# Expert items turned: the last output product behind the next gather, a loop without a drain, the scatter in halves, and part of the routing behind the first gather

## The reference, cut to what matters

```python
def moe_swiglu(xn, w_router, w_gate, w_up, w_down):
    logits = (xn @ w_router).astype(jnp.float32)
    top_v, top_i = lax.top_k(logits, TOP_K)
    top_w = jax.nn.softmax(top_v, axis=-1)
    gates = jnp.sum(jax.nn.one_hot(top_i, N_EXPERTS, dtype=jnp.float32) * top_w[..., None], axis=-2)
    y = jnp.zeros_like(xn)
    for e in range(N_EXPERTS):
        y = y + gates[..., e:e + 1] * swiglu(xn, w_gate[e], w_up[e], w_down[e])
    return y
...
        h = h + moe_swiglu(xn, ...)
        h = h + per_layer_embedding(h, p[i], norm_ple[i], w_ple_up[i], w_ple_gate[i])
```

## Time and profile before

| | |
|---|---|
| median of 3 executions | 2706.61 us (2705.66 to 2718.25) |
| the profiled execution, its own time | 2699.85 us |
| its span, first to last instruction | 2698.0 us |
| mean granted TensorE clock | 0.98 |
| TensorE matmul busy | 2526.2 us, 94% of the span |
| VectorE busy | 1883.0 us, 70% |
| ScalarE busy | 1465.1 us, 54% |
| experts, first expert product to the first product of the next layer | 643.5 to 1693.0 us |

### The profile page before, as it was taken

One profiled execution on the slowest core, in us unless ns is written; L12 is line 12 of the kernel. 1 busy time (PEld: TensorE's weight loads), 2 busy tenths in 40 slices (PEclk: granted clock), 3 DMA queues, 4 the chain that ended last, 5 costly groups with the idle time before them and its releaser, 6 DMA issues.

```text
span 2698.0 us, 32714 instructions
## 1 busy us (share of the span) xinstructions
PE 2526.2 (94%) x13559; PEld 2136.9 (79%) x13559; DVE 1883.0 (70%) x1959; ACT 1465.1 (54%) x1353; POOL 0.2 (0%) x4
## 2 busy tenths in 40 slices
PE   7998998986999999999999898899889999998999
PEld 6977997865888887888888676688668988875898
DVE  5655556447888888888888686658665565767654
ACT  4443334544767676666666575455654344555432
POOL 0000000000000000000000000000000000000000
PEclk9999999998999999999999999999989999998999
DMA  7544854338989898999999795255234545523453
GB/s 239 189 140 144 227 187 140 125 110 293 368 324 369 322 371 322 351 343 351 341 349 345 286 337 182 83 164 172 78 110 158 193 151 166 172 78 101 164 189 125
DMA packets 301812, 597.59 MB, mean 221 GB/s; under 512 B 13552, under 2 KB 105952, under 8 KB 301664
## 3 DMA queue, kind: packets, MB, share of 16 engines
q1 hardware_dynamic: 301664, 595.50, 63.9%
HBM read 594.41 MB, written 1.05 MB: 221 GB/s over the span
## 4 chain that ended last, share of the span: by engine, by line
PE 81%; DVE 11%; ACT 4%; issue 2%; DMA 1%; SPq 0%; DVEq 0%; ACTq 0%
PE ps L211 80%; DVE ring_rounded L705 3%; ACT high_rounded L692 2%; DVE arena_rounded L2040 1%; PE ps L1788 1%; DMA ring<-in_w_down_dense 1%; DVE arena L2525 0%; DVE h L890 0%; DVE arena L2655 0%; DVE ring_rounded L2040 0%; ACT arena L1318 0%; DVE xT_rounded L646 0%; DVE xT L640 0%; DMA ring<-in_w_in_a 0%; PE ps L1298 0%
## 5 line engine op out<-in xcount | busy, mean ns | idle before, releaser
L211 PE MATMUL ps<-high_rounded,arena_rounded 128*128 128x512 f32 x2664 | 830.4, 393 | 20.7 <-DVE arena_rounded L715 8.1
L705 DVE TENSOR_TENSOR ring_rounded<-ring,high_rounded 128x2048 fp32r<-128x2048 f32 (+3 forms) x231 | 513.2, 2230 | 289.9 <-ACT high_rounded L692 288.9
L692 ACT ACTIVATE high_rounded<-ring 128x2048 fp32r<-128x2048 f32 (+3 forms) x231 | 430.4, 1864 | 365.3 <-PE ps L211 339.0
L211 PEld LDWEIGHTS ps<-high_rounded,arena_rounded 128*128 128x128 f32 x2664 | 494.5, 188 | 125.2 <-DVE arena_rounded L715 9.0
L211 PE MATMUL ps<-ring_rounded,arena_rounded 128*128 128x512 f32 x1000 | 392.1, 392 | 0.0
L211 PE MATMUL ps<-xT_high_rounded,high_rounded 128*128 128x256 f32 x1280 | 362.2, 283 | 14.7 <-DVE xT_rounded L646 8.4
L211 PE MATMUL ps<-xT_high_rounded,ring_rounded 128*128 128x256 f32 x1280 | 360.1, 281 | 0.0
L211 PE MATMUL ps<-xT_rounded,high_rounded 128*128 128x256 f32 x1280 | 360.0, 281 | 0.0
L211 PE MATMUL ps<-arena_rounded 128*128 128x512 f32 x864 | 339.2, 393 | 0.0
L2040 DVE TENSOR_TENSOR arena_rounded<-arena,high_rounded 128x2048 fp32r<-128x2048 f32 x131 | 297.2, 2287 | 27.6 <-ACT high_rounded L1843 27.4
L1843 ACT ACTIVATE high_rounded<-arena 128x2048 fp32r<-128x2048 f32 x131 | 251.0, 1919 | 84.6 <-PE ps L211 83.1
(11 more groups left out here) (279 smaller groups left out, 3043.3 us busy)
## 6 DMA issues: line engine op xcount, KB each, us to landing
arena<-in_w_down_moe SPq DMA_DIRECT2D x76, 1024.0 KB, 5.2
arena<-in_w_up_moe SPq DMA_DIRECT2D x72, 1024.0 KB, 5.9
arena<-in_w_gate_moe SPq DMA_DIRECT2D x68, 1024.0 KB, 5.2
ring<-in_w_in SPq DMA_DIRECT2D x50, 1024.0 KB, 5.1
ring<-in_w_gate_moe SPq DMA_DIRECT2D x44, 1024.0 KB, 5.3
ring<-in_w_up_moe SPq DMA_DIRECT2D x40, 1024.0 KB, 5.6
ring<-in_w_down_moe SPq DMA_DIRECT2D x36, 1024.0 KB, 5.1
ring<-in_w_up SPq DMA_DIRECT2D x32, 1024.0 KB, 5.4
```

What stands on the lines that cost most here:

```text
L211: return self.pe.matmul(out, lhsT, rhs, start=start, stop=stop, skip_group_check=True)
L692: act.activation(as_rounded(m, m.highs[n % HIGHS][:, 0:size]), m.slots[n % RING][:, 0:size], ACT.Copy).then_inc(m.rounded, 1)
L705: dve.tensor_tensor(as_rounded(m, slot), slot, as_rounded(m, m.highs[n % HIGHS][:, 0:size]), ALU.subtract).then_inc(m.slabs_split, 1)
```

## The change

Seven edits:

1. Item boundary. The order of the slabs in an item is now the same for straight code and loop (`ITEM_ORDER`), and an item begins with the end of the one before: transpose of its last step, gather of the new item, the last two down slabs of the old one, then gate of the new one. The loop's item begins in the same way, so nothing is emptied before it; the last item is finished behind the loop.
2. The register load of the item count moves on TensorE and VectorE from ahead of the first item to just ahead of the loop (on ScalarE too), and each loads a second register (`last_of`) behind the loop.
3. Scatter. The sums are scaled by the slot's share as they leave PSUM (`slot_share`), split in a high part (ScalarE) and a low part (`vector_shared`, two new VectorE instructions), and scattered by rounded products: 2 of 512 columns per piece, 8 in all. Two pieces stand in step 1 and two in step 2, behind up. The low part lies in the buffer of `xg`.
4. The transposes of `pick` move from step 2 to step 3, and two plain float32 matmuls of 8 columns are added to get the share per slot.
5. High buffers. A fixed table (`HIGH_ORDER`) instead of the running number modulo 5: twelve of an item's 42 slabs (14 to 25) now reuse the buffer of four slabs before, the others of five (one of them later still).
6. Start. VectorE splits three instead of four slabs ahead of the routing, and the plan (`vector_plan`) and the fourth slab stand behind the first gather's split.
7. Behind the experts. VectorE signals each half of `h` as soon as its two pieces are added; one of the two slabs of the next layer is split behind that, the other behind the norm's diagonals (`late`). TensorE makes the norm's products ahead of the embedding's transposes, here and in the first embedding layer.

```diff
-    m.y = a.take(D)
+    m.y_high = a.take(D)
+    m.y_low = m.xg.rearrange("p c n -> p (c n)")
...
         dve.tensor_scalar(out, x, rstd, None, ALU.mult).then_inc(m.xn_ready, L.up(m.xn_ready))
+    if late:
+        vector_lows(dve, L, m)
...
+HIGH_ORDER = [n % 5 for n in range(10)] + [n % 4 for n in range(12)] + [n % 5 for n in range(20)]
...
+    def high(self, pos):
+        return self.m.moe_highs[HIGH_ORDER[pos % ITEM_SLABS]]
+    def freed(self, pos):
+        back = 1
+        while HIGH_ORDER[(pos - back) % ITEM_SLABS] != HIGH_ORDER[pos % ITEM_SLABS]:
+            back += 1
+        return pos - back + 1
...
-def tensor_scatter(pe, L, m):
-    for b in range(4):
+def tensor_scatter(pe, L, m, t):
+    for b in (2 * t, 2 * t + 1):
         pe.wait_ge(m.my.drained, L.room(m.my))
         bank = L.bank(m.my)
-        for n in range(2):
-            col = (b % 2) * 512 + n * 256
-            ins = L.mm(bank[:, n * 256:(n + 1) * 256], m.pickT[:, b // 2, :], m.y[:, col:col + 256])
-            if n:
-                ins.then_inc(m.my.full, L.up(m.my.full))
-            else:
-                L.give_back(ins)
+        chosen, at = as_rounded(m, m.pickT[:, b // 2, :]), slice((b % 2) * 512, (b % 2 + 1) * 512)
+        L.give_back(L.mm(bank, chosen, as_rounded(m, m.y_high[:, at]), True, False))
+        L.mm(bank, chosen, as_rounded(m, m.y_low[:, at]), False, True).then_inc(m.my.full, L.up(m.my.full))
...
 def tensor_experts(pe, L, m):
...
-    items = items_of(pe, m)
     pe.wait_ge(m.v.drained, L.emptied(m.v))
     L.returned = m.m_read
     tensor_items(pe, L, m, ExpertRun(m, 0, FIXED))
+    items = items_of(pe, m)
+    per = {m.ma.full: 8, m.mv.full: 8, m.my.full: 12}
     with pe.Fori(FIXED, items) as turn:
-        L.enter(turn, {m.ma.full: 8, m.mv.full: 8, m.my.full: 12, m.m_read: ITEM_SLABS})
+        L.enter(turn, per, FIXED)
         tensor_items(pe, L, m, ExpertRun(m, turn, 1))
     L.leave()
+    last = last_of(pe, m)
+    L.enter(last, per, 0)
+    tensor_expert_down(pe, L, m, ExpertRun(m, last, 1), STEPS_MOE, tensor_expert_turn(pe, L, m))
+    pe.wait_ge(m.m_acc_drained, 2 * items)
+    for half in range(2):
+        tensor_scatter(pe, L, m, half)
+    L.leave(False)
...
+def tensor_expert_turn(pe, L, m):
...
+def tensor_expert_down(pe, L, m, run, g, turned):
+    hidden = (as_rounded(m, m.m_h_high), as_rounded(m, m.m_h_low))
+    item, s = (g - 1) // STEPS_MOE, (g - 1) % STEPS_MOE
+    pe.wait_ge(m.my.drained, turned)
+    if s == 0 and not (run.opening and item == 0):
+        pe.wait_ge(m.m_acc_drained, 2 * (run.first + item))
+    for half in range(2):
+        tensor_expert_products(pe, L, m, run, (g - 1, "down", half), [m.ps[:, 0, :], m.ps[:, 1, :]], hidden,
+                               s == 0 and half == 0, s == STEPS_MOE - 1 and half == 1)
...
 def tensor_items(pe, L, m, run):
...
-    for g in range(steps + 1):
+    for g in range(run.n * STEPS_MOE):
...
+        follows = g > 0 or not run.opening
+        if s == 0:
+            if follows:
+                turned = tensor_expert_turn(pe, L, m)
+            pe.wait_ge(m.m_picks, run.first + (item + 1))
+            tensor_gather(pe, L, m, 0, m.mv)
+            tensor_gather(pe, L, m, 1, m.my)
+            if follows:
+                tensor_expert_down(pe, L, m, run, g, turned)
+            pe.wait_ge(m.m_xg, run.first + (item + 1))
+        tensor_expert_up(pe, L, m, run, g, "gate", m.ma)
+        if s:
+            turned = tensor_expert_turn(pe, L, m)
+        if s == 3:
...
-        if s == STEPS_MOE - 1 and g + 1 < steps:
...
-            tensor_gather(pe, L, m, 0, m.mv)
-            tensor_gather(pe, L, m, 1, m.my)
...
-    pe.wait_ge(m.m_acc_drained, 2 * (run.first + run.n))
-    tensor_scatter(pe, L, m)
...
+                L.give_back(pe.transpose(bank[:, t * P:(t + 1) * P], m.pick[:, t, :], m.ident))
+            for t in range(TT):
+                ins = L.mm(bank[:, TT * P:TT * P + 8], m.pickg[:, t, :], m.c("ones")[:, 0:8], t == 0, t == 1)
+            ins.then_inc(m.ma.full, L.up(m.ma.full))
+        tensor_expert_up(pe, L, m, run, g, "up", m.mv)
+        if s in (1, 2) and (item or not run.opening):
+            pe.wait_ge(m.m_acc_drained, 2 * (run.first + item))
+            tensor_scatter(pe, L, m, s - 1)
+        if s:
+            tensor_expert_down(pe, L, m, run, g, turned)
...
+def scalar_expert_highs(act, m, run, g, kinds, halves=(0, 1)):
...
+            if not run.opening or run.freed(pos) > 0:
+                act.wait_ge(m.m_read, run.first * ITEM_SLABS + run.freed(pos))
+            act.activation(as_rounded(m, run.high(pos)), run.slot(pos), ACT.Copy).then_inc(m.m_rounded, 1)
...
+def scalar_expert_sums(act, m, item):
+    act.wait_ge(m.m_sums, 2 * item)
+    for n in range(2):
+        act.activation(as_rounded(m, m.y_high[:, n * 512:(n + 1) * 512]), m.ps[:, n, :], ACT.Copy,
+                       scale=m.slot_share[:, 0:1]).then_inc(m.m_y_high, 1)
...
+        follows = item or not run.opening
+        if s == 0 and follows:
+            scalar_expert_highs(act, m, run, g, ("gate",), (0,))
+            scalar_expert_turned(act, L, m)
+            scalar_expert_highs(act, m, run, g, ("gate",), (1,))
+            scalar_expert_highs(act, m, run, g, ("up",))
+            scalar_expert_sums(act, m, run.first + item)
+        elif s:
+            scalar_expert_turned(act, L, m)
+        if s == 0:
...
+            act.activation(as_rounded(m, m.pickT).rearrange("p t n -> p (t n)"), bank[:, 0:TT * P], ACT.Copy)
+            act.activation(m.slot_share, bank[:, TT * P:TT * P + 8], ACT.Copy).then_inc(
+                m.ma.drained, L.up(m.ma.drained))
...
+    act.sem_inc(m.ma.drained, CREDIT)
+    scalar_items(act, L, m, fixed)
...
+    dve.tensor_scalar(m.seat[:, :, 0:EXPERTS], m.posm, -1.0, None, ALU.add).then_inc(m.vector_step, L.up(m.vector_step))
+    dve.wait_ge(m.vector_step, L.at(m.vector_step))
+    dve.tensor_copy(m.share[:, :, 0:EXPERTS], m.gates).then_inc(m.vector_step, L.up(m.vector_step))
+    dve.wait_ge(m.vector_step, L.at(m.vector_step))
+def vector_plan(dve, L, m):
...
+def vector_shared(dve, m, item):
+    for n in range(2):
+        dve.wait_ge(m.m_y_high, 2 * item - 1 + n)
+        at = slice(n * 512, (n + 1) * 512)
+        dve.scalar_tensor_tensor(as_rounded(m, m.y_low[:, at]), m.ps[:, n, :], m.slot_share[:, 0:1],
+                                 as_rounded(m, m.y_high[:, at]), ALU.mult, ALU.subtract).then_inc(m.m_acc_drained, 1)
...
 def vector_items(dve, L, m, run):
...
-        if s == 4 and item + 1 < run.n:
-            vector_picks(dve, m, item + 1)
-        if s == STEPS_MOE - 1 and g + 1 < steps:
-            vector_gathered(dve, L, m, item + 1)
-        vector_expert_lows(dve, m, run, lows)
-    vector_scattered(dve, L, m)
+        follows = item or not run.opening
+        if s == 0 and follows:
+            vector_expert_turned(dve, L, m, run.first * STEPS_MOE + g)
+            vector_expert_lows(dve, m, run, g, ("gate",), (0,))
+            vector_gathered(dve, L, m, run.first + item)
+            vector_expert_lows(dve, m, run, g, ("gate",), (1,))
+            vector_expert_lows(dve, m, run, g, ("up",), (0,))
+            dve.wait_ge(m.m_xg, run.first + (item + 1))
+            vector_shared(dve, m, run.first + item)
+            vector_expert_lows(dve, m, run, g, ("up",), (1,))
+        elif s:
+            vector_expert_turned(dve, L, m, run.first * STEPS_MOE + g)
+        if s + 1 < STEPS_MOE:
+            vector_expert_lows(dve, m, run, g + 1, ("gate",), (0,))
+        else:
+            vector_expert_lows(dve, m, run, g, ("down",), (0,))
...
+        dve.tensor_tensor(m.m_s, m.m_s, bank, ALU.mult).then_inc(m.mv.drained, L.up(m.mv.drained))
+        if s == 3:
+            L.up(m.ma.drained)
+        if s in (1, 2) and follows:
+            vector_scattered(dve, L, m, s - 1)
+        if s == 4:
+            vector_picks(dve, m, run.first + (item + 1))
+        if s + 1 < STEPS_MOE:
+            vector_expert_lows(dve, m, run, g + 1, ("gate",), (1,))
+            vector_expert_lows(dve, m, run, g + 1, ("up",))
+            vector_expert_lows(dve, m, run, g, ("down",))
+        else:
+            vector_expert_lows(dve, m, run, g, ("down",), (1,))
...
-    vector_expert_lows(dve, m, fixed, fixed.splits(fixed.groups[0]))
+    vector_expert_lows(dve, m, fixed, 0, ("gate",))
+    vector_expert_lows(dve, m, fixed, 0, ("up",), (0,))
     vector_route(dve, L, m)
-    items = items_of(dve, m)
...
     vector_picks(dve, m, 0)
     vector_gathered(dve, L, m, 0)
+    vector_expert_lows(dve, m, fixed, 0, ("up",), (1,))
+    vector_plan(dve, L, m)
     vector_items(dve, L, m, fixed)
+    items = items_of(dve, m)
...
+    last = last_of(dve, m)
+    L.enter(last, per, 0)
+    vector_expert_turned(dve, L, m, items * STEPS_MOE)
+    vector_shared(dve, m, last + 1)
+    for t in range(TT):
+        vector_scattered(dve, L, m, t)
+        dve.wait_ge(m.my.drained, L.at(m.my.drained))
```

(13 more changed lines are left out.)

274 lines of the change are left out of this document (98 added, 176 removed).

## The result

The changed kernel takes 2667.35 us (median of 4, 2665.65 to 2669.49) against 2707.1 us (median of 4) before: ratio 0.9844, with its 95% interval in brackets [0.9828, 0.986]. A second set gave 2666.12 against 2708.43, ratio 0.9844 [0.9831, 0.9858]. The forecast was 2674 in 2662 to 2687, faster.

The account below looks back on a forecast made before the run. TensorE, ending 81% of the chain, was taken as the bound. Terms -9.0 - 12.0 - 12.4 + 1.4 - 1.0 + 0.3 = -32.7 us took the median 2706.61 to 2674, range 2662 to 2687.

Parts of the forecast that it names:

- Start: At the start of the experts, picks, gather and first product come 9.0 us earlier; bounds -7 to -10.
- In-item scatter: Scatter inside an item, six times: 2.0 us gained each, bounds 1.0 to 2.8; term -12.0.
- Into the loop with its additions: At the loop's entry: -12.4 us, bounds -10 to -14; small matmuls and the load behind the loop add +1.4.
- Behind the experts: Behind the last item: norm's sums 2.2 us earlier, ScalarE becomes late; term -1.0, bounds 0 to -3.
- First embedding layer: In the first embedding layer, transposes leave an idle stretch and come behind the norm: +0.3 us.
- Sum: All terms together: -32.7 us, giving 2674 from the runs' median of 2706.61.
- Loads: Rival, 7%: in the items the loads become the bound, the scatter's twelve us vanish: 2686.
- Loop entry: Rival, 6%: at the loop's entry, branch, register load and computed waits cost TensorE most of the drain's cost: 2686.
- Buffers: Rival, 7%, half of it slower: four high buffers too few for slabs 14 to 25; 2712 at 0.4 us each.
- More than I count: Rival, 8%: no boundary waits, plan quite covered, end at -3, clock high sooner in the start: 2664.

Follow-up runs that it names:

- the second profile: The changed kernel run again unchanged and profiled a second time: 2666.12 us.
- run 9: The kernel before, with four items in straight code and four loop turns instead of seven and one: 2743.2 us.
- experiment 11: The changed kernel with ScalarE's roundings and VectorE's splits reordered behind the experts and in step 0 of each item: 2661.45 us, ratio 0.9834.
- Experiment 4: The changed kernel with its end undone: both low parts ahead of h, the embedding's transposes ahead of the norm in both layers: 2676.25 us.
- experiment 8: The changed kernel with four items in straight code and four loop turns instead of seven and one: 2670.51 us.
- experiment 6: The changed kernel with thirty-two instead of twelve slabs of each item sharing four high buffers: 2669.27 us.
- experiment 7: The changed kernel with the twelve slabs of each item that share four high buffers sharing three: 2733.3 us, ratio 1.0094.

## Why the prediction was right, term by term

- **Start, -9.0: measured -7.3 to -7.9 by the first expert product, -6.3 to -7.3 with the half clock behind it.** The steps are those foreseen: the routing starts 2.1 earlier (from router product to the small products 3.7 us in the second profile, 5.85 before), and 6.4 us of plan and register load are gone, where I counted 6.8. The rest, 0.8 to 1.2, I put down to the clock, which no run here holds still: it is at half from about the router product to the gather in every profile, and what it covers shifts.
- **In-item scatter, -12.0 (2.0 each): measured -13.5 (2.25 each).** The scatter takes 2.1 us (2.2 assumed), the two small products 0.37 (0.46); the wait shows as 0.24 (0.3 to 0.4 assumed) and costs 0.5. Mechanism and size right.
- **Into the loop with its additions, -12.4 + 1.4 = -11.0: measured -28.06 + 13.5 = -14.6.** This is the term that was mis-sized; it lies outside its bounds (-10 to -14, so -8.6 to -12.6 with the additions). The runs give it a cleaner form: 12.1 for the drain (run 9) and 2.25 for a boundary of the new form, 14.35. In my working the two register loads (0.9) cost nothing, since they run under products already issued, the small products cost 0.16 less, and the loop's item before held one more wait behind the drain that I had not looked for, 0.64 us for the split of a transpose. Of the other 1.9 of the 3.6 us some 0.8 would be, as an estimate, the 0.27 hidden in each wait (experiment 11), which I counted neither at the wait of 1.48 nor at that of 0.64 nor at the ends of the 15.65; 1.1 us stay open. The row of that wait, TensorE of before:

```profile
1574.93 0.73 PE L211 MATMUL ps<-xT_high_rounded,arena_rounded 128*128 128x512 f32 x2 [0.64 <-DVE arena_rounded L2052]
```

- **Behind the experts, -1.0: measured -1.9 to -2.8.** Five of the seven profiles with this end show -2.7 to -2.8. ScalarE did become what is late, as said, and the norm's sums come 2.3 us earlier behind ScalarE's copy, as counted (2.2). I had charged the late slab and the diagonal too much: from the sums to the layer's first product 8.51 us pass against 9.00 before, where my figures made it 1.2 longer. Experiment 4 shows that +1.8 for the split sums and the new scatter and -3.7 to -4.5 for the reordering make the term up.
- **First embedding layer, +0.3: 0.03** by the rows (4.19 to 4.22 us from the norm's first product to the layer's).
- **Sum: -32.7 against -38.2 by rows and -37.0 at like clock**; 2674 against 2667. The sum is nearer than its parts by chance: the start gave 1.7 us less than its term, the others together 7.2 more. That I set the sum beside a median and not beside the lucky profile was right.
- **The rivals.** Loads: no; 125.62 and 124.81 us an item at 352 GB/s and more. The Trainium skill, "DMA: Bandwidth & Descriptors", section "Where 436 GB/s comes from", gives 358 GB/s for a core's share. The trace does not agree that loads are held to it here, with one core at work: the 386 GB/s over 4 us and the 368 GB/s over a slice of 66.6 us stand above it. So the 123.0 us estimated from that figure are no bound that a run bears out; whether an item could go under them none shows. Loop entry: no (experiment 8). Buffers: no (experiment 6), and experiment 7 shows that with three for twelve slabs they cost 66 us, more than the whole gain. "More than I count" (2664) is what happened in part, and not for its reasons: the items and the end came near its terms though the boundary waits stayed, the start did not, and the largest excess, 3.6 us into the loop, is not among them.

## What to carry to other kernels

Where an engine's pipeline is emptied at every turn of a loop, carry the last product into the next turn, behind the first work that can cover its latency: taking back the swap at the boundary alone cost as much as all the edits together had gained, and with it a turn of the loop costs no more than straight code. Price a stall by what disappears when it is gone, not by the idle time in the row (0.24 shown was 0.52, 4.32 shown was 4.85). And before comparing two profiles that lie 0.3% apart, compare their granted clocks in code that did not change.
